# The triangular inverse of an RWKV-7 layer on one core: half of the chunks change partition halves at each doubling level

## The reference, cut to what matters

```python
def rwkv7_scan(r, w, k, v, kk, a):
    def step(S, inp):
        r_t, w_t, k_t, v_t, kk_t, a_t = inp
        sa = jnp.einsum("bhij,bhj->bhi", S, -kk_t)
        S = (S * w_t[:, :, None, :] + sa[..., None] * (kk_t * a_t)[:, :, None, :]
             + v_t[..., None] * k_t[:, :, None, :])
        return S, jnp.einsum("bhij,bhj->bhi", S, r_t)
```

## Time and profile before

| | us |
|---|---|
| median of 3 runs | 1480.11 (1479.02 to 1481.74) |
| the profiled execution | 1479.12 |
| its span | 1477.4 |
| busy TensorE matmul | 1413.9 (96%) |
| busy TensorE weight load | 1081.4 (73%) |
| busy VectorE | 733.7 (50%) |
| busy ScalarE | 510.4 (35%) |
| busy GpSimd | 140.8 (10%) |

### The profile page before, as it was taken

The page is one execution under the profiler, slowest core; times in us unless marked ns, Lnnn a source line. Parts: engine busy times, 40 slices in busy tenths (PEclk is TensorE's granted clock), DMA queues, the critical chain, the costliest instruction groups (busy, mean ns, idle before and its releaser), DMA issues.

```text
span 1477.4 us, 27757 instructions
## 1 busy us (share of the span) xinstructions
PE 1413.9 (96%) x12013; PEld 1081.4 (73%) x12013; DVE 733.7 (50%) x1290; ACT 510.4 (35%) x876; POOL 140.8 (10%) x271
## 2 busy tenths in 40 slices
PE   7999999999999999999999999999999998989996
PEld 7988989998899999998889987874343333333332
DVE  4584957667457556545453443653243242223325
ACT  5543434333255555445454344512111110101003
POOL 8010010201200000000000000011111011110100
PEclk9999999999999999999999999999999999999998
DMA  8552333434194544447536508587999999999996
GB/s 244 179 169 63 123 117 109 130 98 142 59 318 143 171 146 140 150 136 251 204 124 218 171 1 271 193 341 271 394 422 421 421 421 420 421 422 421 421 413 224
DMA packets 161360, 351.01 MB, mean 238 GB/s; under 512 B 13825, under 2 KB 111707, under 8 KB 138331
## 3 DMA queue, kind: packets, MB, share of 16 engines
q1 hardware_dynamic: 161242, 349.30, 64.2%
HBM read 347.18 MB, written 2.10 MB: 236 GB/s over the span
## 4 chain that ended last, share of the span: by engine, by line
PE 82%; DMA 8%; DVE 6%; issue 2%; ACT 1%; SPq 0%; POOL 0%; DVEq 0%; POOLq 0%; ACTq 0%
PE banks L905 20%; PE banks L1440 12%; PE banks L1280 11%; PE banks L898 8%; DMA expert_unit<-in_moe_w_down_dram 7%; PE banks L1300 6%; PE banks L1476 6%; PE banks L1518 3%; DVE piece L2133 2%; PE banks L925 1%; PE banks L1079 1%; PE banks L1411 1%; PE banks L1325 1%; PE banks L1348 1%; PE banks L1061 1%
## 5 line engine op out<-in xcount | busy, mean ns | idle before, releaser
L905 PE MATMUL banks<-hidden_lo_chunks,piece 128*128 128x256 f32 x928 | 262.9, 283 | 0.0
L1440 PE MATMUL banks<-expert_unit,pair_entries 128*64 128x512 f32 x1024 | 240.6, 615 | 22.3 <-issue 21.5
L1702 ACT CAST piece<-arena_fixed 128x1024 fp32r<-128x1024 f32 (+1 forms) x158 | 161.3, 1033 | 178.1 <-PE banks L905 138.2
L2133 DVE TENSOR_TENSOR piece<-arena_fixed,piece 128x1024 fp32r<-128x1024 f32 (+1 forms) x158 | 192.0, 1239 | 54.6 <-ACT piece L1702 54.2
L1440 PEld LDWEIGHTS banks<-expert_unit,pair_entries 128*64 128x64 f32 x1024 | 72.5, 140 | 161.4 <-issue 161.4
L905 PE MATMUL banks<-hidden_hi_low_chunks,piece 128*128 128x256 f32 x928 | 179.9, 292 | 0.0
L905 PE MATMUL banks<-hidden_hi_high_chunks,piece 128*128 128x256 f32 x928 | 178.3, 291 | 0.6 <-DVE hidden_lo_chunks L2116 0.6
L905 PEld LDWEIGHTS banks<-hidden_lo_chunks,piece 128*128 128x128 f32 x928 | 177.8, 192 | 0.0
L2405 DVE TENSOR_TENSOR loop_split<-arena_fixed,loop_split 128x2048 fp32r<-128x2048 f32 x48 | 107.9, 2288 | 111.7 <-ACT loop_split L1869 111.7
L905 PEld LDWEIGHTS banks<-hidden_hi_low_chunks,piece 128*128 128x128 f32 x928 | 145.0, 192 | 6.4 <-issue 3.6
L2664 DVE TENSOR_TENSOR arena_phases<-arena_phases,banks 128x512 f32<-128x512 f32 x128 | 81.8, 682 | 134.9 <-PE banks L1518 134.9
(11 more groups left out here) (406 smaller groups left out, 2043.9 us busy)
## 6 DMA issues: line engine op xcount, KB each, us to landing
expert_unit<-in_moe_w_gate_dram SPq DMA_DIRECT2D x60, 1024.0 KB, 22.6
expert_unit<-in_moe_w_up_dram SPq DMA_DIRECT2D x60, 1024.0 KB, 25.0
expert_unit<-in_moe_w_down_dram SPq DMA_DIRECT2D x52, 1024.0 KB, 22.4
arena_fixed<-in_w_in_dram SPq DMA_DIRECT2D x22, 2048.0 KB, 9.3
arena_fixed<-in_wk_mem_dram SPq DMA_DIRECT2D x8, 2048.0 KB, 8.7
arena_fixed<-in_wv_mem_dram SPq DMA_DIRECT2D x8, 2048.0 KB, 9.0
arena_fixed<-in_w_out_dram SPq DMA_DIRECT2D x8, 2048.0 KB, 8.1
arena_fixed<-in_wq_mem_dram SPq DMA_DIRECT2D x8, 2048.0 KB, 8.1
```

Source lines behind the costliest of these rows:

```text
L905: mm = pe.matmul(b[:, half * T:half * T + T], w(w_)[:, k % 8, :], hidden_x(x_, c), start=c + t == 0 and n > 0, stop=c == NC - 1 and t == 2 ...
L1440: mm = pe.matmul(bank[b][o, :].rearrange("p (g n) -> p g n", g=2), hs_pair[:, c, o], gate_up_unit(i(e))[:, :, c % (NC // 2), :], start=c = ...
L1702: nc.scalar.copy(piece_half(p, 0), raw_piece(p)).then_inc(piece_hi, 1)
L2133: V.tensor_tensor(piece_half(p, 1), raw_piece(p), piece_half(p, 0).bitcast(F32), ALU.subtract)\
```

## The change

The turned inverse of a chunk moves to the other partition half at the levels in which the chunk stands in `FLIPPED`: two of the four chunks each time. After level 5 every chunk has moved an even number of times. P, `Ps`, the inverse and the turned inverse are kept at places that follow from this (`away`, `inverse_at`, `turned_inverse_at`). The products of step 5 are issued so that one chunk that stays and one that moves take turns.

The identity is added to P on its way out of PSUM, on VectorE. So (I + P) times the old inverse is the new one whole, and the two adds become copies: the inverse is copied by ScalarE, the turned one by VectorE. P and step 5 share a pair of banks, steps 3 and 4 have a pair each, and the three pairs (2-3, 4-5, 6-7) change roles from level to level. The wait for the ScalarE copy of step 4 moves from the next level's P to its step 3. In VectorE's program a level now reads Ps, gap, copy of step 5, gap; in ScalarE's copy of step 3, copy of step 4, gap, gap.

```diff
+        FLIPPED = ((0, 1), (0, 2), (1, 2), (0, 1), (0, 1))
+        def away(lv, c):
+            return sum(c in chunks for chunks in FLIPPED[:lv - 1]) % 2
+        def inverse_at(lv, c, pi):
+            return 4 * (pi ^ away(lv, c)) + c if lv else 2 * c + pi
+        def turned_inverse_at(lv, c, pi):
+            if lv == 0:
+                return 2 * c + pi
+            same = c in FLIPPED[lv - 1]
+            return 4 * same + 2 * sum((d in FLIPPED[lv - 1]) == same for d in range(c)) + pi
+        def level_banks(lv):
+            return [2 + 2 * ((lv - 1 + i) % 3) for i in range(3)]
@@ TensorE
                 for lv in LV:
-                    if lv > 1:
-                        pe.wait_ge(*act_rw.at(TURNED[lv - 2](g)))
+                    p_bank, x_bank, turned_bank_ = level_banks(lv)
...
-                        pe.wait_ge(*dve_rw.at(("X", g, lv - 1, 0)))
-                    for k in range(8):
-                        for r, o in SIDES[k % 2]:
-                            mm = pe.matmul(b2(2 + k % 2, 8)[o, k // 2, :], AM[r, k // 4, k % 4, :],
-                                           X[r, 0, k // 4, k % 4, :], start=True, stop=True)
+                        pe.wait_ge(*act_rw.at(("X", g, lv - 1, 0)))
+                    for c in range(NCH):
+                        for pi in range(2):
+                            e, s = divmod(inverse_at(lv, c, pi), 4)
+                            for h in range(2):
+                                r, o = HEADS[h ^ pi], HEADS[h ^ away(lv, c)]
+                                mm = pe.matmul(b2(p_bank + e, 8)[o, s, :], AM[r, c // 2, 2 * (c % 2) + pi, :],
+                                               X0_[r, inverse_at(lv - 1, c, pi), :], start=True, stop=True)
                     mm.then_inc(*pe_rw.mark(("P", g, lv)))
                     gap()
-                    pe.wait_ge(*act_rw.at(("Ps", g, lv)))
+                    pe.wait_ge(*dve_rw.at(("Ps", g, lv)))
                     if lv > 1:
                         pe.wait_ge(*dve_rw.at(("X", g, lv - 1, 1)))
+                        pe.wait_ge(*act_rw.at(TURNED[lv - 2](g)))
...
-                    for k in range(8):
-                        for r in HEADS:
-                            mm = pe.matmul(b2(7, 8)[r, k, :], Ps[r, k // 4, k % 4, :], X[r, 1, k // 4, k % 4, :],
-                                           start=True, stop=True)
+                    flipped_last = [[c for c in range(NCH) if (c in FLIPPED[lv - 1]) == f] for f in (False, True)]
+                    for c_pair in zip(*flipped_last):
+                        for pi in range(2):
+                            for c in c_pair:
+                                e, s = divmod(turned_inverse_at(lv, c, pi), 4)
+                                for h in range(2):
+                                    r, o = HEADS[h ^ away(lv, c)], HEADS[h ^ away(lv + 1, c)]
+                                    mm = pe.matmul(b2(p_bank + e, 8)[o, s, :], Ps_[r, inverse_at(lv, c, pi), :],
+                                                   X1_[r, turned_inverse_at(lv - 1, c, pi), :], start=True, stop=True)
                     mm.then_inc(*pe_rw.mark(("X", g, lv, 1)))
@@ ScalarE
                 for lv in LV:
-                    act.wait_ge(*pe_rw.at(("P", g, lv)))
-                    nc.scalar.copy(odd_even(Ps), two_banks(2, 4 * CH))\
-                        .then_inc(*act_rw.mark(("Ps", g, lv)))
-                    gap()
                     if lv < 5:
+                        _, x_bank, turned_bank_ = level_banks(lv)
+                        act.wait_ge(*pe_rw.at(("X", g, lv, 0)))
+                        nc.scalar.copy(X[:, 0].rearrange("p a b c -> p a (b c)"), banks[:, x_bank:x_bank + 2, 0:4 * CH])\
+                            .then_inc(*act_rw.mark(("X", g, lv, 0)))
...
                         act.wait_ge(*pe_rw.at(TURNED[lv - 1](g)))
...
                             .then_inc(*act_rw.mark(TURNED[lv - 1](g)))
+                    gap()
                     gap()
@@ VectorE
                 for lv in LV:
+                    p_bank = level_banks(lv)[0]
+                    halves = banks[:, p_bank:p_bank + 2, 0:4 * CH]
+                    dve.wait_ge(*pe_rw.at(("P", g, lv)))
+                    V.tensor_tensor(Ps, halves.rearrange("p e (m c) -> p e m c", c=CH),
+                                    bc(id64.unsqueeze(1).unsqueeze(1), 2, NCH, CH), ALU.add).then_inc(*dve_rw.mark(("Ps", g, lv)))
                     gap()
-                    for i in range(2):
-                        if lv == 5 and i == 0:
-                            continue
-                        dve.wait_ge(*pe_rw.at(("X", g, lv, i)))
...
-                            ins = V.tensor_tensor(o, o, two_banks(4, 4 * CH), ALU.add)
...
-                            ins = V.tensor_tensor(o, o, bank[7][:, :], ALU.add)
-                        ins.then_inc(*dve_rw.mark(("X", g, lv, i)))
+                    dve.wait_ge(*pe_rw.at(("X", g, lv, 1)))
+                    V.tensor_copy(X[:, 1].rearrange("p a b c -> p a (b c)"), halves).then_inc(*dve_rw.mark(("X", g, lv, 1)))
                     gap()
```

## The result

| | before | after |
|---|---|---|
| median of 17 runs each, us | 1479.42 (1477.63 to 1481.74) | 1484.32 (1479.91 to 1488.14) |
| ratio after to before | | 1.0029 (95%: 1.0021 to 1.0038) |
| profiled execution, us | 1479.12 | 1479.91 |

The change makes the kernel slower by some 0.3%; forecast were 1484.1 us and "slower". The profiled execution of after happens to be the fastest of its 17, so its rows tell where time goes, and the medians how much. The two profiled executions are only 0.8 us apart. From P of level 1 to the first product of the chunk chain the four groups take 92.7 us before and 94.8 after, 2.1 more; what the medians have beyond that stands in no trace.

A forecast was written before the change was run, and what follows sets the result against it. The prediction took TensorE, busy 96% of the span, to bound the kernel. Its terms, -7.9 + 9.15 + 1.2 + 1.5 = +3.9 us, gave 1483.1 for the profiled execution and 1484.1 us for the median, range 1476 to 1489.

The forecast's parts named there:

- A: Turned-inverse burst through four quarters of the array: 0.52 for 0.90 us in levels 1 to 4, 7.9 us less in sum.
- all on TensorE's path: Claim that the 7.9 us saved in the turned-inverse bursts fully shorten TensorE's time, if other waits allow 3.40 us a level.
- B: Ps queued behind a weight piece on VectorE: TensorE loses 1.83 us each in five counted levels, +9.15 us.
- shrink by 0.38: Rival that bursts stay at 0.90 us: A gone, each stall of B 0.38 us shorter, about 1490 us; chance 0.04.
- my 1.48 and not 1.83: TensorE's loss per level in B: 1.48 us without VectorE and GpSimd taking turns, 1.83 with it.
- C: Level 1, pieces freed before the loop: 2.27 us lost on Ps in groups 0 and 3; +1.2 us net, all groups.
- D: Three TensorE stalls for instructions, 2.20, 1.29 and 2.36 us, in groups 0, 1 and 3, get longer: +1.5 us.
- the end of such a stall follows the load: Assumption in D: an instruction stall ends with the 2 MB weight load, which follows a VectorE piece; +0.5 us each.
- a sign of being wrong: Named as wrong: pieces ahead of Ps without a wait on TensorE, or issue stalls that are gone or new.
- the pieces are covered: Rival: VectorE's delay from weight pieces ahead of Ps does not reach TensorE; 1475.0 us, faster; chance 0.17.
- The fall of the clock: Rival: new idle stretches in level 1 and a longer third stall bring two more clock falls, +3.4, 1487.5 us; chance 0.14.
- My bound for it: Claim that the clock falls from an idle time between 2.20 and 2.36 us on, or somewhat less.

The follow-up runs named there:

- e2: Changed kernel with no chunk ever moving, so the turned-inverse burst goes from each half to the same half; 1488.8 us.
- e1: Changed kernel with VectorE forming the weight pieces held ahead of the next level's Ps only behind that Ps, in levels 2 to 5; 1479.0 us.
- e6: Kernel before with only one change: VectorE and not ScalarE copies P to Ps; 1488.3 us.
- e10: Changed kernel with four weight loads behind the levels and pieces behind Ps in levels 2 to 5, but ahead of Ps in level 1; 1470.0 us.
- e11: Kernel before with three weight loads behind the levels, and Ps copied by VectorE in place of ScalarE; 1479.1 us.

## Why the prediction was right, and where it was not

**A, the burst**, is right as a duration: 0.51 for 0.90. As a gain, undoing it is worth 7.2 us in the levels of the changed kernel's traces and 4.5 in medians, but only 3.1 and 1.2 in the kernel where nothing else waits. What failed there is "all on TensorE's path": instructions come no faster, and four bursts in a row then outrun them. I had named the instruction supply only as something that moves with the loads. The stalls of B do not shrink by 0.38 without A either: in `e2` the two of group 2 are 1.70 and 1.68 us. The piece starts 4.71 us after P in both kernels, but GpSimd comes later behind the slow burst, and the piece takes 2.04 us for 1.68.

**B, Ps behind a piece**, is the mechanism, and the order of events came out almost to the tenth: for group 2 I laid the piece's end 6.38 us after P and TensorE's start at 7.12; P of level 1 is at 269.52, the piece ends at 275.91 and L1102 starts at 276.57, 7.05 after. The sum was too high: 9.15 us against some 5.7 in five waits (1.69, 1.68, 1.24, 0.72 and 0.40; the one in group 3 is covered, as said). Two reasons. Behind level 4 GpSimd has no further masked matrix to make, so the wait in group 1 is 1.24 with a piece of 1.23 us: that is near my 1.48 and not 1.83. And the waits of 0.72 and 0.40 come just behind the stretches at half clock, which I take to let TensorE come late to them; where no such stretch lay just ahead, the same waits are 1.70 (`e2`, groups 0 and 1).

**C, level 1**: laid at 2.27 us lost, found as idle times of 2.08 and 1.96, with the add's wait gone. In groups 1 and 2 nothing is lost.

**D** has a step that failed in the mechanism: "the end of such a stall follows the load". In group 0 the load was issued 0.6 us later after P of level 1 than before, as I laid it, and the stall ended 0.9 us earlier. It ends 2.5 us behind a packet of instructions, at 106.78 and 109.26, while the load lands at 112.95. In group 3 the load is 0.6 us later and the end 1.6 earlier. The three stalls are where they were, of 1.44, 2.01 and 1.19 us instead of 2.20, 1.29 and 2.36, and new ones came, two of them of 1.23 and 1.06 us; new stalls are what I had named as a sign of being wrong. The term is right in size by luck: +1.5 forecast, 5.8 to 7.3 us measured. That loads bring the large ones was inferred then and is shown now.

**The rivals.** That the pieces are covered is out (`e1`, `e6`). The fall of the clock did come: two stretches in after's trace for one before, and over all runs a mean clock of 0.988 against 0.990. Over 1480 us that difference could be worth some 3 us (an estimate), of the 4.9 that the medians show. No run here moves the clock alone, so its size stays open. My bound for it was wrong: the two falls came behind idle times of 1.44 and 2.01 us, and the 2.08 us in level 1 brought one in `e6`, `e10` and `e11` and none in after, so the length of one idle time does not decide it.

**The total** was hit by luck to a good part. With the forecast -7.9 for the bursts, the traces have +9.8 for the waits on Ps, -2.5 for the add and +1.4 for issue, which is +0.8 us in all; the levels grew by 2.1, and the second stretch at half clock can cost at most 1.7. B was 3.4 us too dear, and what stands in its place in the medians is most likely the clock, which my sum had left out.

## What to carry to other kernels

Before moving a short operation to another engine's queue, look at what stands ahead of it in program order: a copy of 0.7 us behind a 1.2 us piece costs TensorE 1.2 to 1.7 us, although VectorE is busy for only half of the time. Put work that is wanted late behind the operation that is waited for; here this alone turned a loss of 4.9 us into a tie. When removed waits come back as "issue", look at when the packets of instructions start and which transfers run beside the dense stretch of small matmuls, and move those.

## What the runs showed of the hardware

- 16 products of 64 x 64 in a row take 0.51 us when each four of them go through all four quarters of the array, and 0.90 when they go from a half to the same half with one output bank, 0.83 with two.
- A VectorE and a GpSimd operation that both have two SBUF inputs take turns: the one that begins second lasts longer by most of the first one's rest (VectorE's 1.22 us becomes 1.68 to 2.12, GpSimd's 1.10 becomes 1.97). A VectorE operation with one input in PSUM keeps its time: Ps at 270.68 took 0.69 us with GpSimd at work from 270.32 to 271.72.
- TensorE's instructions come in packets of 16,384 bytes, about one for 256 of its records, and every idle time with no releaser in the levels ends where a new 256 begin, 2.3 to 2.9 us after a packet started. Beside a 2 MB load the packet starts later, and TensorE stood 0.3 to 3.3 us; with no load near, 0.2 to 1.0 us. Moving three such loads behind the levels was worth 7.8 us.
- TensorE's clock fell to 1.2 GHz at idle times of 1.4 to 3.3 us, but not at each of them: 2.08 us in the same place brought a fall in three kernels and none in four.
